# One masked decay matrix in place of two: POOL masks the exponents of a state-space stage, and the sums of squares use four column groups

## What is computed

```python
def ssd_chunked(xs, dt, A, Bm, Cm, h0):
    ...
    acum = jnp.cumsum(a, axis=-1)
    tri = jnp.tril(jnp.ones((Q, Q), dtype=bool))
    seg = jnp.exp(jnp.where(tri, acum[..., :, None] - acum[..., None, :], -jnp.inf))
    cb = jnp.einsum('bclgn,bcsgn->bcgls', Cc, Bc)
    y_diag = jnp.einsum('bcgrls,bcsgrp->bclgrp', cb[:, :, :, None] * seg, xdt)
    ...
    y_off = jnp.einsum('bclgn,bcgrpn,bcgrl->bclgrp', Cc, h_prev, jnp.exp(acum))
    y = (y_diag + y_off)
...
    def finish(y_f, y_b, xs, z):
        y = y_f + flip(y_b) + D_skip[:, None] * xs
        return rmsnorm(y * jax.nn.silu(z), norm_w) @ out_w
```

## Time and profile before

| | before |
|---|---|
| median of 3 runs | 2228.65 us (2225.99 to 2233.58) |
| span of the profiled execution | 2228.2 us |
| busy: PE, DVE, ACT, POOL | 2031.3 (91%), 972.5 (44%), 648.4 (29%), 72.4 (3%) us |
| mean granted clock of PE | 0.978 |
| group loop of the state-space stage | about 640 to 997 us |
| its output product | about 1002 to 1093 us |
| first expert layer of the second block | from 1094 us |

### The profile page before, as it was taken

How to read it: one execution, slowest core, us unless ns; L and a number is a source line. 1 busy time by engine, 2 the same in 40 slices (tenths; PEclk the granted TensorE clock), 3 DMA queues, 4 the chain that set the end, 5 groups by cost and what they waited for, 6 DMA issues and landing times. The chain is left out here.

```text
span 2228.2 us, 25120 instructions
## 1 busy us (share of the span) xinstructions
PE 2031.3 (91%) x10198; PEld 1076.7 (48%) x10198; DVE 972.5 (44%) x1668; ACT 648.4 (29%) x1284; POOL 72.4 (3%) x106
## 2 busy tenths in 40 slices
PE   6987987999899999999899999988899899999887
PEld 5844444444377888878643333322345422222222
DVE  4687224454688888882522221222466400001002
ACT  4243123111277667762211111100226111111100
POOL 0101010000000000000000000000120000000000
PEclk9998998999899999999999999999999999999999
DMA  8547567899433433322669999999830499999997
GB/s 291 204 147 264 189 248 291 341 397 382 125 97 95 131 115 114 110 99 76 281 265 428 427 428 427 427 427 429 332 147 1 175 428 426 427 425 427 426 426 300
DMA packets 147321, 623.57 MB, mean 280 GB/s; under 512 B 15460, under 2 KB 66151, under 8 KB 109063
## 3 DMA queue, kind: packets, MB, share of 16 engines
q1 hardware_dynamic: 142288, 601.65, 67.8%
q0 software_dynamic: 2352, 16.91, 2.0%
q10 hardware_dynamic: 2566, 3.41, 0.5%
HBM read 620.76 MB, written 1.18 MB: 279 GB/s over the span
## 5 line engine op out<-in xcount | busy, mean ns | idle before, releaser
L2907 PE MATMUL bank<-slots,xgTe 128*64 128x512 f32 (+1 forms) x1664 | 373.2, 595 | 31.9 <-DMA slots<-in_moe_w 31.8
L3128 DVE TENSOR_TENSOR actse<-sge,bank 32x512 f32<-32x512 f32 (+1 forms) x48 | 32.8, 682 | 498.0 <-PE bank L2907 278.8
L2907 PEld LDWEIGHTS bank<-slots,xgTe 128*64 128x64 f32 (+1 forms) x1664 | 107.5, 124 | 273.4 <-issue 229.0
L2907 PE MATMUL bank<-slots,aTe 128*64 128x512 f32 (+1 forms) x704 | 165.2, 612 | 13.9 <-issue 13.9
L3025 ACT ACTIVATE sge<-bank 32x512 f32<-32x512 f32 (+1 forms) x48 | 28.3, 590 | 480.3 <-PE bank L2907 480.1
L516 PE MATMUL bank<-slots_r 128*128 128x512 f32 x416 | 163.4, 393 | 0.0
L515 PE MATMUL bank<-hT_r,slots_r 128*128 128x512 f32 x384 | 155.6, 405 | 0.0
L517 PE MATMUL bank<-slots_r 128*128 128x512 f32 x384 | 152.0, 396 | 0.0
L585 PE MATMUL bank<-slots,hT 128*128 128x512 f32 (+1 forms) x320 | 133.2, 578 | 4.5 <-DVE hT L482 3.0
L2907 PEld LDWEIGHTS bank<-slots,aTe 128*64 128x64 f32 (+1 forms) x704 | 48.6, 129 | 113.9 <-issue 113.9
L3037 ACT ACTIVATE aTe<-bank 128x512 f32<-128x512 f32 x32 | 19.1, 597 | 275.2 <-PE bank L2964 275.2
(11 more groups left out here) (571 smaller groups left out, 3159.0 us busy)
## 6 DMA issues: line engine op xcount, KB each, us to landing
slots<-in_moe_w SPq DMA_DIRECT2D x148, 2048.0 KB, 26.2
slots<-in_ada_w SPq DMA_DIRECT2D x24, 2048.0 KB, 12.1
extra0e<-in_moe_w SPq DMA_DIRECT2D x23, 2048.0 KB, 26.4
slots<-in_ssd_in_w SPq DMA_DIRECT2D x48, 512.0 KB, 5.3
slots<-in_moe_w_gate SPq DMA_DIRECT2D x23, 1024.0 KB, 10.4
slots<-in_moe_w_up SPq DMA_DIRECT2D x23, 1024.0 KB, 12.4
slots<-in_moe_w_down SPq DMA_DIRECT2D x23, 1024.0 KB, 7.4
rowsB<-acum_rows POOLq DMA_DIRECT2D x16, 1024.0 KB, 5.9
```

The costliest lines, as they stand in the source:

```text
L2907: i = pe.matmul(bank[64 * n:64 * n + NJ * CAP, :], lhsT(4 * h + k), wv[:, 0, n * 512:(n + 1) * 512], start=(h == 0 and k == 0), stop=(h == ...
L3128: i = dve.tensor_tensor(acts[r_, :], sg[r_, :], psum[1][r_, :], ALU.mult)
```

## The change

POOL gets two `affine_select` a group, one per direction, on the loaded rows in place, after ACT's carried exponentials: outside the direction's triangle the row value becomes -1e30, so its exponential is 0. They take the place of DVE's two clips; ACT's 16 exponentials a direction now wait for them (`outside_masked` for `clipped`). The B and C product is copied once, unmasked. After both directions' exponentials DVE adds the two directions (per stream, two instructions) and multiplies the sum with the unmasked product (per stream, two instructions), each of which raises `m_ready`; the mask product in the middle of DVE's group is gone. PE makes one diagonal product per chunk and head, and waits for the first stream's half before chunk 0 and for the second's before chunk 2. The squares' sums put two tiles times two streams on four groups of 32 columns, each over 256 columns; `ssum` is half as wide, and the last sum picks the stream's half of the partitions.

```diff
@@ sum_squares (PE)
-                    for j in range(2):
-                        i = pe.matmul(b.ap[64 * j:64 * j + 64, :], const("ones")[:, 0:64], gate_buf(2 * q + j), start=True,
-                                      stop=True, tile_position=(0, 64 * j), skip_group_check=True)
+                    for j in range(2):
+                        for s_ in range(2):
+                            row = 64 * s_ + 32 * j
+                            i = pe.matmul(b.ap[row:row + 32, 0:S], const("ones")[:, 0:32],
+                                          gate_buf(2 * q + j)[:, s_ * S:(s_ + 1) * S], start=True,
+                                          stop=True, tile_position=(0, row), skip_group_check=True)
@@ outputs (PE)
-                    pe.wait_ge(m_ready, 2 * g + 2)
                     for t in range(TT):
+                        if t % NT == 0:
+                            pe.wait_ge(m_ready, 2 * g + 1 + t // NT)
                         tt = slice(t * P, (t + 1) * P)
-                        terms = [(d, None) for d in range(2)]
+                        terms = [(0, None)]
...
-                                    left, right = tok[:, t, hd], rowsB[:, d, h, tt]
+                                    left, right = tok[:, t, hd], rowsB[:, 0, h, tt]
@@ POOL
+                    for d, step in enumerate((1, -1)):
+                        pool.wait_ge(ea_done, 2 * g + d + 1)
+                        r = rowsB[:, d, :, :].rearrange("p h (t n) -> p (h t) n", t=TT)
+                        pool.affine_select(r, r, [[0, HPG * TT], [step, P]], ALU.is_ge, far_below, base=0,
+                                           channel_multiplier=-step).then_inc(outside_masked, 1)
@@ decay (ACT)
-                    act.wait_ge(clipped, 2 * g + d + 1)
+                    act.wait_ge(outside_masked, 2 * g + d + 1)
@@ DVE
-                def clip(g, d):
-
-                    dve.wait_ge(ea_done, 2 * g + d + 1)
-                    r = rowsB[:, d, :, :].rearrange("p h (t n) -> p h t n", t=TT)
-                    a_s = acs[:, :, d * 32 + g * HPG:d * 32 + (g + 1) * HPG].rearrange("p t h -> p h t")
-                    dve.tensor_tensor(r, r, a_s.unsqueeze(3).broadcast_to([P, HPG, TT, P]), ALU.min).then_inc(clipped, 1)
...
-                def mask_decay(g, d):
-
-                    dve.wait_ge(exps_out, 2 * g + d + 1)
-                    r = rowsB[:, d, :, :]
-                    dve.tensor_tensor(r, r, cbm[:, d, :].unsqueeze(1).broadcast_to([P, HPG, TT * P]),
-                                      ALU.mult).then_inc(m_ready, 1)
+                def join_decays(g):
+
+                    dve.wait_ge(exps_out, 2 * g + 2)
+                    stream_of = [slice(s_ * S, (s_ + 1) * S) for s_ in range(2)]
+                    for c in stream_of:
+                        i = dve.tensor_tensor(rowsB[:, 0, :, c], rowsB[:, 0, :, c], rowsB[:, 1, :, c], ALU.add)
+                    link(i)
+                    for c in stream_of:
+                        dve.tensor_tensor(rowsB[:, 0, :, c], rowsB[:, 0, :, c],
+                                          cbm[:, c].unsqueeze(1).broadcast_to([P, HPG, S]), ALU.mult).then_inc(m_ready, 1)
...
-                    for d in range(2):
-                        mask = const(("upto", "from")[d]).unsqueeze(1).broadcast_to([P, TT, P])
-                        i = dve.tensor_tensor(cbm[:, d, :].rearrange("p (t n) -> p t n", t=TT),
-                                              b.ap[:, :].rearrange("p (t n) -> p t n", t=TT), mask, ALU.mult)
-                    i.then_inc(emptied[DVE], 1)
+                    dve.tensor_copy(cbm, b.ap[:, :]).then_inc(emptied[DVE], 1)
```

More of the change, by code:

```diff
@@ L2077, in build @@
             tok = carve(TT * 384).rearrange("p (t n) -> p t n", t=TT)
-            cbm = carve(2 * TT * P).rearrange("p (d n) -> p d n", d=2)
+            cbm = carve(TT * P)
             cea_at = pos[0]
@@ L2090, in build @@
                                 else hT_r[:, i - 8, :])
-            ssum = w_dt[:, :, :].rearrange("p k n -> p (k n)")
+            ssum = w_dt[:, :, :].rearrange("p k n -> p (k n)")[:, 0:S]
             assert pos[0] <= SLOTS * SLOT
@@ L2104, in build @@
                 "dt_loaded", "edges_zeroed", "rows_loaded"))
-            (clipped, conv_done, silu_done, skip_done, ea_done, exps_out, cea_ready, m_ready, prod_ready, hp_ready) = (sem(x) for x in (
-                "clipped", "conv_done", "silu_done", "skip_done", "ea_done", "exps_out", "cea_ready", "m_ready", "prod_ready", "hp_ready"))
+            (outside_masked, conv_done, silu_done, skip_done, ea_done, exps_out, cea_ready, m_ready, prod_ready, hp_ready) = (sem(x) for x in (
+                "outside_masked", "conv_done", "silu_done", "skip_done", "ea_done", "exps_out", "cea_ready", "m_ready", "prod_ready", "hp_ready"))
             z_used, y_squared, y_rounded, y_split, y_summed, y_rooted = (sem(x) for x in (
@@ L2303, in _ @@
                             for t_ in range(TT):
-                                i = pe.matmul(b.ap[:, t_:t_ + 1], ssum[:, t_ * P:(t_ + 1) * P], const("ones")[:, 0:1],
+                                stream_rows = (const("upto")[:, 63:64], const("from")[:, 64:65])[t_ // NT]
+                                i = pe.matmul(b.ap[:, t_:t_ + 1], ssum[:, t_ % NT * P:(t_ % NT + 1) * P], stream_rows,
                                               start=True, stop=True, skip_group_check=True)
@@ L2321, in _ @@
                 norm.pool(pool)
+                far_below = pool.to_reg(-BIG)
                 pool.wait_ge(emptied[DVE], banks["acumT"].done)
@@ L2604, in sum_batch @@
                     if q == 0:
-                        dve.tensor_copy(ssum, b.ap[:, :]).then_inc(emptied[DVE], 1)
+                        dve.tensor_copy(ssum, b.ap[:, 0:S]).then_inc(emptied[DVE], 1)
                     else:
                         dve.wait_ge(emptied[DVE], banks["ss", q - 1].done)
-                        dve.tensor_tensor(ssum, ssum, b.ap[:, :], ALU.add).then_inc(emptied[DVE], 1)
+                        dve.tensor_tensor(ssum, ssum, b.ap[:, 0:S], ALU.add).then_inc(emptied[DVE], 1)
                 def add_output(g):
@@ L2617, in add_output @@
                         dve.tensor_tensor(y, y, b.ap[:, :], ALU.add).then_inc(emptied[DVE], 1)
-                def clip(g, d):
-                    dve.wait_ge(ea_done, 2 * g + d + 1)
-                    r = rowsB[:, d, :, :].rearrange("p h (t n) -> p h t n", t=TT)
-                    a_s = acs[:, :, d * 32 + g * HPG:d * 32 + (g + 1) * HPG].rearrange("p t h -> p h t")
-                    dve.tensor_tensor(r, r, a_s.unsqueeze(3).broadcast_to([P, HPG, TT, P]), ALU.min).then_inc(clipped, 1)
                 def carry_c(g):
                     for d, runs in enumerate((((P, 0, 384),), ((0, 0, P), (2 * P, P, 256)))):
+                        dve.wait_ge(ea_done, 2 * g + d + 1)
                         for at, to, n in runs:
@@ L2663, in _ @@
                     i.then_inc(prod_ready, 1)
-                    clip(g, 0)
-                    clip(g, 1)
                     if more and g:
@@ L2672, in _ @@
                     carry_c(g)
-                    dve.wait_ge(emptied[DVE], banks["cbs", g].done)
-                    mask_decay(g, 0)
                     if more:
@@ L2691, in _ @@
                     dve.sem_inc(hp_ready, 1)
-                    mask_decay(g, 1)
+                    dve.wait_ge(emptied[DVE], banks["cbs", g].done)
+                    join_decays(g)
                     if more:
@@ L2714, in _ @@
                 dve.wait_ge(sst_full, 1)
-                dve.tensor_scalar(eps_rows[:, 0:TT], b.ap[:, 0:TT], 1.0 / 64, None, ALU.mult).then_inc(sst_taken, 1)
+                dve.tensor_scalar(eps_rows[:, 0:TT], b.ap[:, 0:TT], 1.0 / 32, None, ALU.mult).then_inc(sst_taken, 1)
                 dve.wait_ge(sst_taken, 1)
```

## The result

The changed kernel takes 2216.16 us, median of 4 runs (2211.68 to 2218.31); the kernel before takes 2231.11 in the runs beside it (2225.99 to 2233.97). The ratio is 0.9941, with a 95% interval of 0.9928 to 0.9953: faster by about 13 to 15 us, where 15.5 were forecast. The profiled executions differ by 13.4 us in span, 2228.2 before and 2214.8 after. In a second set of five runs the same kernel took 2215.05 beside 2230.07, ratio 0.9936 (0.9923 to 0.9950).

What follows compares the result with a forecast made beforehand. PE was taken to bound the state-space loop, with DVE close behind. Output products 14.0, squares' sums 4.0, first and last group 0.8, less 3.3 for selects, gave 15.5 us: 2228.65 to 2213.1 us, range 2206 to 2229.

Steps and rivals of the forecast that it cites:

- output products: PE: 16 fewer matmuls a group at 0.109 us each, 1.75 us a group, 14.0 us over 8 groups.
- squares' sums: PE: four column groups overlap, a batch takes 0.5 us instead of 1.0, saving 4.0 us over 8 batches.
- selects, middle groups: POOL's selects make DVE 1.8 us late against 1.25 us slack; six group transitions lose 3.3 us.
- first and last group: DVE there: selects not covered, but both clips leave the chain; 0.4 us won each, 0.8 us together.
- The bound: State-space loop: PE bounds it, DVE close behind; the stage's gain reaches the end one for one, nothing later absorbing it.
- A: Length of one POOL select over 128x2048, taken as 2.5 us, with 1.8 to 4.6 kept for the range.
- D: DVE's delay in a middle group from two back-to-back selects: 2A - 3.2, forecast as 1.8 us.
- the slack: Middle groups: lead of the ACT and DVE chain over PE, 1.25 us at squares and tokens, 2.4 at output products.
- selects fully covered: Rival: A at or under 2.1, or DVE not stopped; gain 21.3 us, time 2207.3; chance 0.27.
- the forecast's own: Main case: A from 2.1 to 3.05, selects partly covered, gain 15.5 us, time 2213.1; chance 0.42.
- DVE's Z lowering starting right where the second select ends: Sign the forecast is right: in a middle group this lowering starts at 796.0, not at ACT's rounding.
- Does a select stop DVE?: POOL against DVE: assumed that selects block DVE's two-input SBUF instructions, as a DVE instruction had held a POOL one.

## Why the prediction was right, step by step

The forecast was 15.5 us; the medians differ by 15.0 (the ratio gives 13.1) and the spans by 13.4. That they agree so closely is luck: within the sum the selects and the first and last group came out 5.1 us better than forecast, the squares' sums and the end of the stage 4.4 us worse, and the two cancelled.

| term | forecast | measured | where it is read |
|---|---|---|---|
| output products | 14.0 | 14.0 | 1.75 a group; cadence 46.01 to 44.26 in the kernel before with one product less |
| squares' sums | 4.0 | 3.5 | 0.57 instead of 1.01 a batch |
| selects, middle groups | -3.3 | 0 | same cadence with and without them |
| first and last group | 0.8 | 2.6 | gap 1.74 to none, 1.54 to 0.69 |
| end of the stage | none | -3.9 | new gap 2.32, clock 1.6 |
| sum | 15.5 | 16.2 | the stage: 16.14 |

**The bound.** PE is busy throughout the loop before and after, and nothing after the stage absorbed its gain at once: by the start of the second expert layer (POOL's first row there), at 1751.45 before and 1734.66 after, 16.8 us were there, 0.4 of them from ahead of the stage, which began at 648.59 and 648.16.

**Output products.** 14.0 held to the tenth, by the one experiment that changes nothing else.

**Squares' sums.** Four column groups overlap. The step took 1.0 less 0.5 us for a batch; the trace has 1.01 and 0.57. That is 0.44 a batch rather than 0.5.

**The select.** This term was mis-sized: A is 2.00, not 2.5, near the lower bound from the memset slope (a memset of this size takes 1.78). The prediction's own rule then gives D = 2 x 2.0 - 3.2 = 0.8, the trace shows DVE delayed by 0.60 (2.89 - 2.29), and both lie inside the slack. The loss of 3.3 is 0. So for the middle groups the case that came true is the one called "selects fully covered", which had a chance of 0.27, and not the forecast's own; its mark, no gap and a cadence of 43.8, is there. Its time, 2207.3, was missed all the same, by the end of the stage. "DVE's Z lowering starting right where the second select ends" did not show: it started at 785.87, at ACT's rounding, and was held for its tail.

**Does a select stop DVE?** Yes, as the step assumed; the convolution of 3.11 took 6.36 beside two selects and the selects 4.79 instead of 3.97. The row it leaned on the earlier trace rows had shown less: there POOL was held, not DVE, and DVE's instruction read one tensor beside a value per partition, not two tensors. It stops both ways: of the last group's selects one took 2.32 and the other 3.51.

```profile
955.75 5.79 POOL L2341 TENSOR_SCALAR_AFFINE_SELECT rowsB<-rowsB 128x2048 f32<-128x2048 f32 x2 [10.91 <-ACT slots L2448]
956.12 5.97 DVE L2635 TENSOR_TENSOR slots<-slots 128x1536 f32<-128x1536 f32 x2
```

**First and last group.** The step had the selects in the way of DVE and a gain of 0.4 each. DVE was stopped, as it said, but shorter selects and the clips' absence closed 1.74 of 1.74 and 0.85 of 1.54. The gap of 0.69 that is left isn't the selects': it is the same 0.69 without them. In the trace the two adds (968.42) follow right behind the state recurrence (its last row 967.52 + 0.69), and PE starts when the first mask product is done, so that chain would set it; that was not tried.

**The step that was missing.** The sum ended at the last group's output products. Behind them DVE has a fixed list: two lowerings, two Y rows, two additions, then gate 15, then ACT's squares. The kernel before has ACT's squares and PE's sums of them 0.6 us apart, 999.35 + 1.24 = 1000.59 and 1001.19:

```profile
999.35 1.24 ACT L2383 ACTIVATE slots<-Yt 128x512 f32<-128x512 f32 x2 [4.26 <-DVE Yt L2508]
...
1001.19 1.08 PE L2175 MATMUL bank<-slots,consts 128*64 128x512 f32 x4
```

The changed kernel has the pair as 982.21 + 1.23 = 983.44 and the 983.49 shown above:

```profile
982.21 1.23 ACT L2394 ACTIVATE slots<-Yt 128x512 f32<-128x512 f32 x2 [4.25 <-DVE Yt L2519]
```

In the last group PE's way from the output products to these sums becomes 2.0 us shorter (10.89 before; 977.33 + 3.84 = 981.17, behind the gating matmuls, less 972.25 after), while that list stays. And the list starts behind both of DVE's mask products (970.81 + 2.36 = 973.17), while the first of them releases PE: counted from PE's output products the squares are ready after 11.19 us, where it was 10.29. A slack of 0.6, used up by 2.0 and by 0.9, leaves the gap of 2.3. The prediction looked for slack in the middle groups only and carried the end along. The kernel before with one product less shows the same wait, 1.1 us, and the new order of DVE's list takes it away, so its cause is that list. The remaining 1.6 us are the clock: with the gap filled by idle matmuls they went, and the gap's end stayed where it was.

**The span.** 16.1 in the stage and 13.4 in the span: the second expert layer took 469.4 us in the profiled execution before and 472.9 after, 3.5 longer. The second profile of the same kernel has 469.5, that without selects 469.8 and that with memsets 473.1. So this is a difference between executions, not of the change; what makes it was not settled. Scatter of that kind is as large as the distance between the two ways of putting the gain, 15.0 and 13.1.

## What to carry to other kernels

As long as nothing waits for its result, an added instruction on a second engine cost here what it overlapped with its neighbour's work, not its length: place it where the neighbour is idle (4 us here), and price it by that window and by the slack behind it. When the bounding engine gets shorter, look for the next one at the end of the loop as well as in its middle: the last iteration has other work queued behind it, and here moving three calls on DVE brought back 3.9 us of gap and clock. When removing a product needs a mask, ask what the mask itself saves: here the move of the clips was worth about 1.3 us of the stage and the joined sum 14.

## What the runs showed of the hardware

A POOL select over 128x2048 fp32 takes 2.00 us, a memset of that tile 1.78, so the select costs 12% more.

A select and a two-input DVE instruction on SBUF hold each other up, and either may be the one that waits: 2.29 became 2.89 on DVE, 2.00 became 3.51 and 4.05 on POOL. The rows are not wholly exclusive: in the first group 3.11 and 3.97 us of work took 6.36 together, from 655.24 to 661.60. A memset and the same DVE work do not: 3.11 stayed 3.11.

A PE gap of 2.3 us can cost more than itself. In the changed kernel's profile PE stood from 981.17 to 983.49, and the next nine 512-column matmuls came about 0.43 us apart, before the rest came 0.23 apart:

```profile
984.46 0.63 PE L516 MATMUL bank<-slots_r 128*128 128x512 f32 x1
...
988.04 0.39 PE L516 MATMUL bank<-slots_r 128*128 128x512 f32 x1
```

Two lengths for the same matmul, 0.63 and 0.39, with a mean granted clock of 0.72 over these 6 us, are TensorE's two levels, 1.2 and 2.4 GHz. The fall was there in the profiles of the changed kernel (twice) and of the kernels without selects, with memsets and with the squares on two groups (a gap of 2.02), and in the stage length each time; in that with the clips on DVE, with a gap of 2.31, it was not, nor in the kernel before with fewer products, with a gap of 1.11. What decides it stays open. Filling the gap with idle matmuls kept the level at 1.00 and was worth those 1.6 us.
